# A first stage that sums the modulation as rows from split weights, and output stages with four half buffers

## The chip, the cores and the metric

One kernel on one core of one Trainium2 chip. The metric is the device time of one execution in microseconds (us), and lower is better. Of several runs the median is given. The engines are TensorE (PE, with its weight loads as PEld), VectorE (DVE), ScalarE (ACT), GpSimd (POOL) and SyncE (SP, which here only issues transfers).

## The reference, cut to what matters

Two layers over 1024 latent tokens (x) and 256 context tokens (ctx), all of width 1024 and in fp32. Each layer modulates its input, mixes the tokens, projects back with an output matrix and normalises.

```
silu_c, silu_cc = silu(c), silu(c_ctx)
sh, sc, g = split(silu_c @ mod_w[layer] + mod_b[layer], 3)      # the same for ctx with silu_cc
u = h * (1 + sc) + sh
y = mixer(u)            # layer 0: convolution and mLSTM; layer 1: latent attention
                        # both end in  (...) @ w_out, with w_out (2048, 1024)
h = layer_norm(ALPHA * h + g * y)
```

Layer 0's gates are columns 9216 to 9231 of u @ ev_w_in, plus ev_gate_b.

## The kernel before, in words

Every fp32 product is made of three matmuls on operands split in a high part (the value rounded to F32R) and a low part (value minus high part): high by high, high by low, low by high (mm3, L36 to L42). ACT writes the high part by a copy or an activation that rounds. DVE subtracts and writes the low part over the raw value.

The program is a row of stages: `stage_modulate` (L73), `stage_even` (layer 0's mixer), `stage_out` for layer 0, `stage_latent` and `stage_attend` (layer 1's mixer), `stage_out` for layer 1. A stage ends with a barrier of all engines, so the next begins when the slowest is through. Inside a stage each engine runs its own list of instructions in the order written, and semaphores tie the lists together.

**The first stage** makes u, transposed (1024 features in eight groups k of 128, on the partitions; 1280 tokens along the row), and the gate rows. The tokens lie in three chunks j: 0 holds the 256 context tokens, 1 and 2 hold 512 each. Per k, in the order of PE:
- `columns(k)` (L249): 32 plain fp32 matmuls, with a 128x128 block of mod_w as the stationary operand and two columns of silu as the moving one, give shift and scale of the 128 features. It waits for the slab of mod_w. DVE adds the bias (L201, whose end is the release of all that follows).
- `turn(k)` (L266): ten transposes of the tokens' 128x128 blocks in rotating banks.
- `gates(k-1)` for chunks 1 and 2; those of chunk 0 all come at the end.

ACT applies scale and shift to each transposed chunk and writes u_hi (L166), for chunk 2 also the unrounded u (L168). DVE writes the unrounded u of chunks 0 and 1 (L208), and subtracts to u_lo for all three (L216). After the last gate matmul ACT moves the gate rows out of their banks (`gate_rows`, L174, L175). SP loads mod_w in slabs of 128 columns, two transfers each, into six buffers (L133); ACT issues the ten token tiles of 4 KB rows (L179) ahead of all its own work. `stage_even` then starts with PE projecting tile (0, 0), while ACT waits for the next weights (L540).

**An output stage** computes y = m @ w_out for `count` blocks of 128 tokens (ten in layer 0, eight in layer 1), with 16 blocks of 128 along the sum, so 16 x 2 x 3 = 96 matmuls of 512 columns for each block. The transposed input m is loaded in two halves of eight (L1094), split by ACT (L1166) and DVE (L1214). It has two buffers of 16. The first two blocks go together while w_out arrives in 16 parts (`first_pair`, L1097, L1170, L1218), and every later block n is `project(n)`. A block's load waits until block n-2 is projected (`load_m`). DVE's order is norm(n), then the split of n+2; ACT's is the split of n+2, then `modulate(n)` (L1181; layer 0 only), which empties the banks of PE's `transposes(n)` (L1311). Those come after project(n+1), and after project(2) both 0 and 1. In layer 0 POOL applies gain and bias to the normalised block (L1152, L1154) and stores it.

Of the kernel before, what the change touches and what calls it, by code (L numbers as in the profile page):

```python
# [9 lines left out]
P = 128  # L10
# [62 lines left out]
def stage_modulate(nc, a, keep):  # L73

    SLOTS, TP, R36 = 6, 4, 36
    u_hi, u_lo, mod_col, ident = keep["u_hi"], keep["u_lo"], keep["mod_col"], keep["ident"]
    gate_i, gate_f = keep["gate_i"], keep["gate_f"]
# [4 lines left out]
    PIECES = [(k, j) for k in range(KD) for j in range(3)]  # L82
    piece_at = numbered(PIECES)
    by_dve = numbered(x for x in PIECES if x[1] < 2)
    GATES = (1, 2, 0)
    with ExitStack() as ctx:
        s = Space(nc, ctx, "m")
        u_raw = over(nc, "m_u_raw", [P, KD, T], F32, keep["u_lo_at"])
        x_tok = [s.sb(f"x_tok{n}", [P, D]) for n in range(NT)]
        w = [s.sb(f"w{b}", [P, KD, 2, P]) for b in range(SLOTS)]  # L90
        c_row, c_tanh = s.sb("c_row", [2 * KD, P]), s.sb("c_tanh", [2 * KD, P])
        gw_raw = s.sb("gw_raw", [P, KD, 16])
        gw_hi, gw_lo = s.pair("gw", [P, KD, P])
        g_pre = s.sb("g_pre", [P, 1])
        tp_bank = [s.bank(f"tp{i}") for i in range(TP)]
        col_bank = [s.bank(f"col{i}") for i in range(2)]
        gate_late = [s.bank(f"gate{i}") for i in range(2)]
        gate_bank = [col_bank[0], *gate_late]
        x_in = [s.sem(f"x_in{j}") for j in range(3)]
        w_in = [s.sem(f"w_in{b}") for b in range(SLOTS)]  # L100
        c_in, ident_in, b_in, gw_in, pre_in, first_in = (s.sem(n) for n in ("c_in", "ident_in", "b_in", "gw_in", "pre_in", "first_in"))
        c_t, c_s, c_tp, c_ok, b_ok, ones_ok = (s.sem(n) for n in ("c_t", "c_s", "c_tp", "c_ok", "b_ok", "ones_ok"))
        cols_done, col_ok, tp = (s.sem(n) for n in ("cols_done", "col_ok", "tp"))
        u_hi_ok, u_raw_a, u_raw_d, u_ok = (s.sem(n) for n in ("u_hi_ok", "u_raw_a", "u_raw_d", "u_ok"))
        gw_zero, gw_hi_ok, gw_ok, gate_done, first_hi = (s.sem(n) for n in ("gw_zero", "gw_hi_ok", "gw_ok", "gate_done", "first_hi"))
        w_src = a["mod_w"][0].rearrange("(k p) n -> p k n", p=P)
        h0_src = a["h0"].rearrange("(n p) d -> n p d", p=P)
# [16 lines left out]
        tp_of = lambda k, j: tp_bank[(piece_at[(k, j)] - 1) % TP]  # L124

        @block.sync
        def _(sp):
            def load_slab(k):
                if k >= SLOTS:
                    sp.wait_ge(cols_done, k - SLOTS + 1)  # L130
                for half in range(2):
                    c = D * half + P * k
                    sp.dma_start(w[k % SLOTS][:, :, half, :], w_src[:, :, c:c + P]).then_inc(w_in[k % SLOTS], 16)  # L133
# [4 lines left out]
            load_slab(0)  # L138
            sp.dma_start(b_col[:, :, :], a["mod_b_col"]).then_inc(b_in, 16)
            load_slab(1)  # L140
            sp.dma_start(gw_raw[:, :, :], a["ev_w_in"].rearrange("a (k p) n -> p (a k) n", p=P)[:, :, G0:G0 + 16]).then_inc(gw_in, 16)
            sp.wait_ge(gw_zero, 1)
# [5 lines left out]
            for k in range(2, KD):  # L148
                load_slab(k)
            sp.dma_start(w_first[:, :, :], a["ev_w_in"].rearrange("a (k p) n -> p (a k) n", p=P)[:, :, 4 * D:4 * D + P]).then_inc(first_in, 16)  # L150

        @block.gpsimd
        def _(pool):
            pool.memset(g_pre[:, :], 0.0).then_inc(gw_zero, 1)
            pool.memset(f(gw_hi[:, :, :]), 0.0).then_inc(gw_zero, 1)
            pool.memset(f(gw_lo[:, :, :]), 0.0).then_inc(gw_zero, 1)

        @block.scalar
        def _(act):
# [1997 lines left out]
```

## Time and profile before

| | |
|---|---|
| median of 3 runs | 3075.17 us (3072.52 to 3076.87) |
| the profiled execution | 3071.61 us |
| its span, first to last instruction | 3069.8 us |
| mean granted TensorE clock | 0.972 |
| PE busy | 2917.5 us (95%) |
| DVE, ACT, POOL busy | 1531.2, 1178.5, 234.9 us |
| moved by DMA | 200.79 MB, mean 65 GB/s |

The first stage ends at about 100 us of the span. Layer 0's output stage runs from 1319 to about 1610 us, layer 1's from 2861 us to the end. Overlapping matmuls are shown with their latency, so the cost of one in a stream is the distance from start to start. A granted clock of 1.00 is 2.4 GHz and 0.50 is 1.2 GHz.

### The profile page before, as it was taken

What the parts mean: (1) busy time and instruction counts of PE and PEld (TensorE: products, weight loads), DVE (VectorE), ACT (ScalarE), POOL (GpSimd) and SP (SyncE); (2) the same over time, 40 slices, a digit from 0 to 9 for tenths busy, and PEclk for the clock granted to TensorE, in tenths of its full rate; (3) what the DMA queues carried; (4) which work ended last, traced back from release to release, by engine and by line L of the source; (5) the groups of instructions that cost most, each with busy time, mean ns of one, the idle gap of its engine ahead of it and who ended that gap; (6) DMA issues with size and microseconds to landing.
All of it is one profiled execution on the core that took longest, in us unless ns stands there. A gap on an engine that the chain in (4) does not pass through costs nothing. (4 is left out here: it accounts for less than half of the span.)

```text
span 3069.8 us, 38485 instructions
## 1 busy us (share of the span) xinstructions
PE 2917.5 (95%) x15623; PEld 2505.9 (82%) x15623; DVE 1531.2 (50%) x2791; ACT 1178.5 (38%) x1971; POOL 234.9 (8%) x275
## 2 busy tenths in 40 slices
PE   7999999999999999979979997999999999999798
PEld 7788888888888788857867886888888888887577
DVE  2625652654365535544432323666666656665353
ACT  2423322331233123322234222666666666665310
POOL 0100000000000000002320000202102012020000
PEclk8899999999999999989989998999999999999799
DMA  6311131113111311153341221000100101100432
GB/s 187 93 33 44 45 114 30 44 52 107 30 46 50 107 30 52 33 204 108 121 146 39 90 96 46 26 28 26 32 25 26 36 18 32 31 19 18 175 110 69
DMA packets 223866, 200.79 MB, mean 65 GB/s; under 512 B 12141, under 2 KB 194301, under 8 KB 223690
## 3 DMA queue, kind: packets, MB, share of 16 engines
q1 hardware_dynamic: 207194, 171.28, 18.5%
q0 software_dynamic: 4656, 16.56, 1.4%
q10 hardware_dynamic: 11840, 10.49, 1.0%
q8 instruction: 125, 2.05, 0.3%
q14 instruction: 51, 0.42, 0.1%
HBM read 157.34 MB, written 40.95 MB: 65 GB/s over the span
## 5 line engine op out<-in xcount | busy, mean ns | idle before, releaser
L40 PE MATMUL v_pj<-e_u_hi,e_w_hi 128*128 128x512 f32 (+1 forms) x864 | 308.7, 357 | 1.9 <-PEq L57 1.9
L40 PE MATMUL v_pj<-e_u_hi,v_w_hi 128*128 128x512 f32 (+1 forms) x864 | 308.6, 357 | 0.0
L41 PE MATMUL v_pj<-e_u_lo,v_w_hi 128*128 128x512 f32 (+1 forms) x864 | 306.7, 355 | 0.0
L41 PE MATMUL v_pj<-e_u_lo,e_w_hi 128*128 128x512 f32 (+1 forms) x864 | 306.7, 355 | 0.0
L42 PE MATMUL v_pj<-e_u_hi,v_w_lo 128*128 128x512 f32 (+1 forms) x864 | 306.5, 355 | 0.0
L42 PE MATMUL v_pj<-e_u_hi,e_w_lo 128*128 128x512 f32 (+1 forms) x864 | 306.5, 355 | 0.0
L40 PE MATMUL o_y_bank<-o_w_hi,o_m_hi 128*128 128x512 f32 x576 | 230.9, 401 | 48.8 <-DVE o_w_lo L1218 31.2
L1840 ACT CAST t_pt_hi<-t_ring 128x512 fp32r<-128x512 f32 (+1 forms) x384 | 181.6, 519 | 237.3 <-PE t_ring L2024 237.3
L1925 DVE TENSOR_TENSOR t_pt_lo<-t_ring,t_pt_hi 128x512 fp32r<-128x512 f32 (+1 forms) x384 | 216.2, 598 | 52.8 <-ACT t_pt_hi L1840 51.4
L41 PE MATMUL o_y_bank<-o_w_lo,o_m_hi 128*128 128x512 f32 x576 | 229.0, 398 | 0.0
L42 PE MATMUL o_y_bank<-o_w_hi,o_m_lo 128*128 128x512 f32 x576 | 228.6, 397 | 0.0
L1851 ACT ACTIVATE t_prob<-t_scores,t_bias 128x1280 f32<-128x1280 f32 x128 | 170.6, 1333 | 104.7 <-DVE t_bias L1941 103.9
L40 PEld LDWEIGHTS v_pj<-e_u_hi,v_w_hi 128*128 128x128 f32 x864 | 163.9, 190 | 23.6 <-issue 2.4
L42 PEld LDWEIGHTS v_pj<-e_u_hi,e_w_lo 128*128 128x128 f32 x864 | 163.8, 190 | 23.1
L40 PEld LDWEIGHTS v_pj<-e_u_hi,e_w_hi 128*128 128x128 f32 x864 | 163.9, 190 | 23.0 <-issue 2.1
L42 PEld LDWEIGHTS v_pj<-e_u_hi,v_w_lo 128*128 128x128 f32 x864 | 163.6, 189 | 23.3
L41 PEld LDWEIGHTS v_pj<-e_u_lo,v_w_hi 128*128 128x128 f32 x864 | 164.0, 190 | 21.0
L41 PEld LDWEIGHTS v_pj<-e_u_lo,e_w_hi 128*128 128x128 f32 x864 | 164.0, 190 | 20.6
L1856 ACT ACTIVATE t_prob<-t_prob,t_rec 128x1280 f32<-128x1280 f32 x128 | 177.1, 1384 | 7.4 <-DVE t_rec L1945 7.4
L40 PEld LDWEIGHTS o_y_bank<-o_w_hi,o_m_hi 128*128 128x128 f32 x576 | 111.2, 193 | 75.2 <-DVE o_w_lo L1218 31.9
L40 PE MATMUL l_pj<-l_u_hi,l_w_hi 128*128 128x512 f32 (+3 forms) x376 | 149.8, 399 | 17.2 <-DVE l_u_lo L1530 17.2
L2024 PE MATMUL t_ring<-k_ident,t_prob 128*128 128x128 f32 x1280 | 161.5, 273 | 3.4 <-ACT t_prob L1856 3.4
(380 smaller groups left out, 6446.5 us busy)
## 6 DMA issues: line engine op xcount, KB each, us to landing
e_w_raw<-in_ev_w_in SPq DMA_DIRECT2D x72, 512.0 KB, 4.7
v_mw<-in_mod_w SPq DMA_DIRECT2D x32, 512.0 KB, 4.3
l_w_raw<-in_od_w_in SPq DMA_DIRECT2D x21, 512.0 KB, 4.0
o_m_raw<-mixT SPq DMA_DIRECT2D x20, 512.0 KB, 5.3
m_w<-in_mod_w SPq DMA_DIRECT2D x16, 512.0 KB, 7.7
o_w_raw<-in_ev_w_out SPq DMA_DIRECT2D x16, 512.0 KB, 10.3
zgT<-l_lat_q POOLq DMA_DIRECT2D x16, 512.0 KB, 3.6
t_zg<-zgT SPq DMA_DIRECT2D x32, 256.0 KB, 2.7
```

The source lines that it names most:

```text
L40: nc.tensor.matmul(out, whi, xhi, start=first, stop=False)
L41: nc.tensor.matmul(out, whi, xlo, start=False, stop=False)
L42: return nc.tensor.matmul(out, wlo, xhi, start=False, stop=last)
L1840: nc.scalar.copy(dst, src).then_inc(ring_hi, 1)
L1851: nc.scalar.activation(prob[x][:, :], S[:, 0:T], ACT.Exp, bias=bias[x][:, :], accum_out=total[x][:, :]).then_inc(exp_ok, 1)
L1856: nc.scalar.mul(prob[x][:, :], prob[x][:, :], rec[x][:, :]).then_inc(prob_ok, 1)
L1925: nc.vector.tensor_tensor(dst, src, hi, ALU.subtract).then_inc(ring_free, frees(op))
L2024: last = nc.tensor.transpose(ps[:, c * P:(c + 1) * P], prob[t % 2][:, (c0 + c) * P:(c0 + c + 1) * P], ident[:, :])
```

## The change

First stage. The modulation is now computed as rows. silu is split in high and low (cs, 4 columns: two variants high, two low) and is the stationary operand; the split weights of the slab are the moving one. 16 F32R matmuls of 256 columns give a [4, 256] sum; DVE copies it out, and two small matmuls with a 4x2 selection matrix turn it to columns and add high and low. For that each slab of mod_w (128 x 2048 elements) is split by ACT (`w_high`) and DVE (`w_low`). Slabs come singly at first, then in pairs, over two buffers of a pair. The tokens are loaded by column spans (features 0 to 255, 256 to 511, 512 to 1023), all by SP. u_lo of chunks 0 and 1 is subtracted by POOL. Each chunk has one transpose bank; the gates of chunk 0 run inside the loop. The gate banks stay alive, and `stage_even`'s ACT empties them as its first work.

Output stages. m has four buffers of half a block. Block 2 is loaded when the first half of the first pair is through, block n > 2 when block n-2 is; each split comes one iteration earlier.

```diff
 def stage_modulate(nc, a, keep):
-            for n in range(NT):
-                act.dma_start(x_tok[n][:, :], h0_src[n]).then_inc(x_in[j], 16)
+            def load_slab(k, count):
+                if k >= 4:
+                    sp.wait_ge(r_done, k - 2)
+                for half in range(2):
+                    c = D * half + P * k
+                    sp.dma_start(w_raw[(k // 2) % 2][:, :, half, P * (k % 2):P * (k % 2) + P * count], w_src[:, :, c:c + P * count]).then_inc(w_in[arrival(k)], 16)
...
+            load_slab(0, 1)
+            sp.dma_start(sel[:, :], a["c_sel"]).then_inc(sel_in, 16)
+            sp.dma_start(b_col[:, :, :], a["mod_b_col"]).then_inc(b_in, 16)
+            load_x(0)
+            load_slab(1, 1)
...
+            load_slab(2, 2)
+            load_x(1)
+            load_slab(4, 2)
+            load_x(2)
+            load_slab(6, 2)
...
         @block.gpsimd
+            for k in range(KD):
+                for j in (1, 0):
+                    pool.wait_ge(u_raw_d, by_dve[(k, j)])
+                    pool.wait_ge(u_hi_ok, piece_at[(k, j)])
+                    pool.tensor_tensor(u_lo[:, k, span(j)], u_raw[:, k, span(j)], f(u_hi[:, k, span(j)]), ALU.subtract).then_inc(u_lo_p, 1)
...
         @block.scalar
+            def u(k):
+                act.wait_ge(col_ok, k + 1)
+                high(k, 1)
+                high(k, 2)
+                whole(k, 2)
+                high(k, 0)
+            def w_high(k):
+                act.wait_ge(w_in[arrival(k)], 32)
+                if k >= 2:
+                    act.wait_ge(r_done, k - 1)
+                nc.scalar.copy(high_of(k), slab(w_raw, k)).then_inc(w_hi_ok, 1)
...
+            w_high(0)
+            u(0)
+            w_high(1)
...
+            w_high(2)
+            for k in range(1, KD):
+                u(k)
+                if k + 2 < KD:
+                    w_high(k + 2)
...
         @block.vector
+            row_sums(0)
             for k in range(KD):
                 columns(k)
                 whole(k, 0)
                 whole(k, 1)
...
+                else:
+                    if k + 1 < KD:
+                        row_sums(k + 1)
+                    low(k, 2)
+                    if k + 2 < KD:
+                        w_low(k + 2)
...
         @block.tensor
+            def row_sums(k):
+                pe.wait_ge(w_lo_ok, k + 1)
...
+                for kk in range(KD):
+                    nc.tensor.matmul(sums, cs[:, kk, :], high_of(k)[:, kk, :, :], start=kk == 0, stop=False)
+                    last = nc.tensor.matmul(sums, cs[:, kk, :], slab(w_lo, k)[:, kk, :, :], start=False, stop=kk == KD - 1)
+                last.then_inc(r_done, 1)
...
+            def turn(k, j):
...
+                if k:
+                    if j == 2:
+                        pe.wait_ge(u_raw_a, k)
+                    elif j == 1:
+                        pe.wait_ge(u_raw_d, by_dve[(k - 1, 1)])
+                    else:
+                        pe.wait_ge(u_hi_ok, piece_at[(k - 1, 0)])
...
+            for k in range(KD):
+                row_sums(k)
+                for j in ORDER:
+                    turn(k, j)
+                if k:
+                    for j in ORDER:
+                        gates(k - 1, j)
+                columns(k)
+            for j in ORDER:
+                gates(KD - 1, j)
 def stage_even(nc, a, keep):
+            for j, bank in enumerate((x_bank, y_bank, z_bank)):
+                gate_rows(j, bank)
             act.wait_ge(const_in, 16)
 def stage_out(nc, a, keep, layer):
-    YB = 3
+    YB, SLOTS = 3, 4
+    HALVES = [(0, 0), (1, 0), (0, 1), (1, 1)] + [(n, h) for n in range(2, count) for h in range(2)]
+    order_of = numbered(HALVES)
+    slot = lambda n, h: (order_of[(n, h)] - 1) % SLOTS
...
             def load_m(n, h):
-                b = n % 2
-                if n >= 2:
-                    sp.wait_ge(y_half, half_at[(n - 2, 1)])
+                b = slot(n, h)
+                if n == 2:
+                    sp.wait_ge(first_half, 1)
+                if n > 2:
+                    sp.wait_ge(y_half, half_at[(max(n - 2, 1), 1)])
...
             for n in range(count):
+                if n + 3 < count:
+                    load_m(n + 3, 0)
+                    load_m(n + 3, 1)
                 if n + 2 < count:
-                    load_m(n + 2, 0)
-                    load_m(n + 2, 1)
                     load_res(n + 2)
...
             for n in range(count):
                 norm(n)
-                if n + 2 < count:
-                    split(n + 2, 0)
-                    split(n + 2, 1)
+                if n + 3 < count:
+                    split(n + 3, 0)
+                    split(n + 3, 1)
...
+                    if k == H - 1:
+                        last.then_inc(first_half, 1)
```

## Rows read from the trace of the kernel before

**Rows 1.** The page's busy time, share and instructions of each engine.
```profile
PE 2917.5 (95%) x15623; PEld 2505.9 (82%) x15623; DVE 1531.2 (50%) x2791; ACT 1178.5 (38%) x1971; POOL 234.9 (8%) x275
```
**Rows 2.** Stretches: length, busy and count per engine, granted clock, DMA share, GB/s.
```profile
30.00:40.00 10.00, 10.00 (x44) 9.61 (x45) 4.20 (x10) 3.74 (x6) 0.00 (x0) 1.00 1.20 291
...
50.00:60.00 10.00, 10.00 (x44) 9.52 (x44) 2.66 (x6) 2.79 (x4) 0.00 (x0) 0.50 0.00 0
```
**Rows 3.** First stage in order of time: start, length, instruction [idle before, releaser].
```profile
20.27 6.96 PE L249 MATMUL m_col<-k_c_silu,m_w 128*128 128x2 f32 x32 [11.86 <-DMA m_w<-in_mod_w]
...
36.11 0.16 DVE L201 TENSOR_TENSOR k_mod_col<-m_col,k_b_col 128x4 f32<-128x4 f32 x1 [4.31 <-PE m_col L249]
...
89.04 2.37 PE L266 MATMUL m_tp<-k_ident,m_x_tok 128*128 128x128 f32 x10
89.21 0.16 DVE L201 TENSOR_TENSOR k_mod_col<-m_col,k_b_col 128x4 f32<-128x4 f32 x1 [3.83 <-PE m_col L249]
```
**Rows 4.** First stage by line and form: count, busy us, mean ns, idle before.
```profile
L249 PE MATMUL m_col<-k_c_silu,m_w 128*128 128x2 f32 x256 | 40.9, 295 | 11.9 <-DMA m_w<-in_mod_w 11.9
...
L166 ACT ACTIVATE e_u_hi<-m_tp,k_mod_col 128x512 fp32r<-128x512 f32 x16 | 12.5, 778 | 2.9 <-PE m_tp L266 2.3
...
L168 ACT ACTIVATE m_u_raw<-m_tp,k_mod_col 128x512 f32<-128x512 f32 x8 | 6.2, 770 | 0.0
...
L166 ACT ACTIVATE e_u_hi<-m_tp,k_mod_col 128x256 fp32r<-128x256 f32 x8 | 4.5, 565 | 42.9 <-PE m_tp L266 42.9
```
**Rows 5.** Order of time, matmuls of 256 columns, last two gates, then stage_even.
```profile
98.29 0.28 PE L41 MATMUL m_col<-e_u_lo,m_gw_hi 128*128 128x256 f32 x1
...
98.41 0.28 PE L42 MATMUL m_col<-e_u_hi,m_gw_lo 128*128 128x256 f32 x1
...
100.60 0.36 PE L40 MATMUL v_pj<-e_u_hi,e_w_hi 128*128 128x256 f32 x1 [1.91 <-PEq L57]
...
102.00 0.41 PE L40 MATMUL v_pj<-e_u_hi,e_w_hi 128*128 128x256 f32 x1
...
102.21 0.41 PE L41 MATMUL v_pj<-e_u_lo,e_w_hi 128*128 128x256 f32 x1
```
**Rows 6.** Input tile of the output stages: count, min/median/max ns, first and last start.
```profile
L1166 ACT CAST o_m_hi<-o_m_raw x36: 1040/1053/1060, 1323.6 to 3022.8; 128x1024 fp32r<-128x1024 f32 x36
L1214 DVE TENSOR_TENSOR o_m_lo<-o_m_raw,o_m_hi x36: 1216/1226/3423, 1324.7 to 3023.9; 128x1024 fp32r<-128x1024 f32 x36
```
**Rows 7.** POOL by line and form: count, busy us, mean ns, idle before.
```profile
L1803 POOL TENSOR_TENSOR t_turn<-t_turn,t_part 128x512 f32<-128x512 f32 x16 | 20.5, 1281 | 24.8 <-DVE t_part L1911 23.7
```
**Rows 8.** ACT in order of time, its first work on weights in stage_even.
```profile
105.85 1.05 ACT L540 CAST v_w_hi<-e_w_raw 128x1024 fp32r<-128x1024 f32 x1 [2.81 <-DMA e_w_raw<-in_ev_w_in]
```
**Rows 9.** Layer 0's output stage, PE in order of time, two starts and their streams.
```profile
1383.04 0.79 PE L40 MATMUL o_y_bank<-o_w_hi,o_m_hi 128*128 128x512 f32 x1 [5.59 <-DVE o_m_lo L1214]
...
1388.30 0.40 PE L40 MATMUL o_y_bank<-o_w_hi,o_m_hi 128*128 128x512 f32 x1
...
1407.13 0.40 PE L42 MATMUL o_y_bank<-o_w_hi,o_m_lo 128*128 128x512 f32 x1
...
1414.20 0.76 PE L40 MATMUL o_y_bank<-o_w_hi,o_m_hi 128*128 128x512 f32 x1 [2.51 <-DVE o_m_lo L1214]
...
1419.01 0.39 PE L42 MATMUL o_y_bank<-o_w_hi,o_m_lo 128*128 128x512 f32 x1
```
**Rows 10.** Layer 1's output stage, PE in order of time, start of project(2).
```profile
2927.56 0.79 PE L40 MATMUL o_y_bank<-o_w_hi,o_m_hi 128*128 128x512 f32 x1 [7.38 <-DVE o_m_lo L1214]
...
2931.35 0.40 PE L40 MATMUL o_y_bank<-o_w_hi,o_m_hi 128*128 128x512 f32 x1
```
**Rows 11.** Layer 0's output stage, DVE: norm(1), first and last instruction.
```profile
1384.13 0.69 DVE L1233 TENSOR_TENSOR o_y<-o_y_bank,o_g_bc 128x512 f32<-128x512 f32 x1
...
1389.50 0.81 DVE L1243 TENSOR_SCALAR o_y<-o_y,o_mean_var,o_rstd 128x1024 f32<-128x1024 f32 x1 [0.94 <-POOL o_rstd L1143]
```
**Rows 12.** Input of both output stages: issue to landing.
```profile
DMA to landing us min/median/max: 3.9/5.3/13.3
```

More of the change, by code:

```diff
@@ L88, in stage_modulate @@
         u_raw = over(nc, "m_u_raw", [P, KD, T], F32, keep["u_lo_at"])
-        x_tok = [s.sb(f"x_tok{n}", [P, D]) for n in range(NT)]
-        w = [s.sb(f"w{b}", [P, KD, 2, P]) for b in range(SLOTS)]
+        x_tok = s.sb("x_tok", [P, NT, D])
+        w_hi = [s.sb(f"w_hi{b}", [P, KD, 2 * P], F32R) for b in range(2)]
+        w_lo, w_raw = [], []
+        for b in range(2):
+            at = next_offset(nc)
+            w_lo.append(s.sb(f"w_lo{b}", [P, KD, 2, 2 * P], F32R))
+            w_raw.append(over(nc, f"m_w_raw{b}", [P, KD, 2, 2 * P], F32, at))
@@ L91, in stage_modulate @@
         c_row, c_tanh = s.sb("c_row", [2 * KD, P]), s.sb("c_tanh", [2 * KD, P])
+        cs = s.sb("cs", [P, KD, 4], F32R)
+        sel = s.sb("sel", [4, 2])
+        rows = s.sb("rows", [4, 2 * P])
         gw_raw = s.sb("gw_raw", [P, KD, 16])
         gw_hi, gw_lo = s.pair("gw", [P, KD, P])
[L94 to L102, printed above, removed]
+        tp_bank = keep["pj"]
+        x_bank, y_bank, z_bank, col_bank = keep["banks"]
@@ L242, in columns @@
             def columns(k):
-                b = k % SLOTS
-                pe.wait_ge(w_in[b], 32 * (k // SLOTS + 1))
-                if k >= 2:
-                    pe.wait_ge(col_ok, k - 1)
+                pe.wait_ge(rows_ok, k + 1)
+                if k:
+                    pe.wait_ge(col_ok, k)
                 for half in range(2):
-                    for kk in range(KD):
-                        last = nc.tensor.matmul(col_bank[k % 2][:, 2 * half:2 * half + 2], w[b][:, kk, half, :], c_silu[:, kk, :],
-                                                start=kk == 0, stop=kk == KD - 1)
+                    last = nc.tensor.matmul(col_bank[:, 2 * half:2 * half + 2], rows[0:4, P * half:P * half + P], sel[0:4, :], start=True, stop=True)
@@ L1057, in stage_out @@
         m_hi, m_lo, m_raw = [], [], []
-        for b in range(2):
-            m_hi.append(s.sb(f"m_hi{b}", [P, KM, P], F32R))
+        for b in range(SLOTS):
+            m_hi.append(s.sb(f"m_hi{b}", [P, H, P], F32R))
             m_at = next_offset(nc)
-            m_lo.append(s.sb(f"m_lo{b}", [P, KM, P], F32R))
-            m_raw.append(over(nc, f"o{layer}_m_raw{b}", [P, KM, P], F32, m_at))
+            m_lo.append(s.sb(f"m_lo{b}", [P, H, P], F32R))
+            m_raw.append(over(nc, f"o{layer}_m_raw{b}", [P, H, P], F32, m_at))
         res = [s.sb(f"res{b}", [P, D]) for b in range(2)]
@@ L1208, in _ @@
         def _(dve):
[L1209 removed]
             def split(n, h):
[L1212 to L1214 removed]
+                b = slot(n, h)
+                dve.wait_ge(m_hi_ok, order_of[(n, h)])
+                nc.vector.tensor_tensor(m_lo[b][:, :, :], m_raw[b][:, :, :], f(m_hi[b][:, :, :]), ALU.subtract).then_inc(m_ok, 1)
             def split_w(k):
@@ L1257, in _ @@
                 split_w(k)
+            split(2, 0)
+            split(2, 1)
             if layer == 0:
@@ L1269, in _ @@
                 norm(n)
-                if n + 2 < count:
-                    split(n + 2, 0)
-                    split(n + 2, 1)
+                if n + 3 < count:
+                    split(n + 3, 0)
+                    split(n + 3, 1)
         @block.tensor
```

225 lines of the change are left out of this document (120 added, 105 removed).

## The prediction

> **What bounds the kernel now.** I read the page's engine line first: PE is busy for 95% of the span [rows 1], so only stretches in which PE stands still, runs slowly, or does work that could be shorter are worth anything. The diff touches the first stage and the two output stages, and I read those in windows, in order of time and by line.
>
> In the first stage PE looks full: 10.00 of 10.00 us in both windows [rows 2]. It isn't at its peak there. The clock is 0.50 from 50 to 60 us, and 256 matmuls of two columns take 40.9 us [rows 4], for a result of four numbers per feature. The stage has a beginning, a period and a tail. The first matmul on mod_w starts at 20.27 us, after waiting 11.86 us for its slab, because ten token tiles share the DMA engines with it [rows 3]. DVE's modulation column is ready at 36.27 us for group 1 and at 89.37 us for group 7 [rows 3], six periods of 8.85 us. The last gate matmul starts at 98.41 us and the next stage's first at 100.60 us [rows 5].
>
> In an output stage the matmuls follow each other closely but for a few places, which the order of time shows. Project(2) starts 5.59 us late in layer 0 and 7.38 us late in layer 1, each time released by the split of its input [rows 9, 10]: the load of block 2 may only start when the first pair is through. Project(3) in layer 0 waits another 2.51 us [rows 9]. After each gap PE runs at half clock for a while.
>
> **The step lengths of PE.** Between 1388.30 and 1407.13 us project(2) issues 83 of its 96 matmuls of 512 columns, 0.227 us each at 2.4 GHz. Its first 12 take 5.26 us from 1383.04, 0.438 each at 1.2 GHz [rows 9]. With 256 columns the distance is 0.12 us at the fast level and 0.21 at the slow one [rows 5].
>
> **First stage, the new period.** Count from the moment when the column of group k is ready. Two chains run to the same moment of group k+1.
>
> The chain of ACT and DVE: u(k) on ACT is two of 0.778, one of 0.770 and one of 0.565, 2.89 us [rows 4]. Then w_high(k+2): the trace has no copy of 2048 elements, so I take two of 1024, 2 x 1.053 = 2.11 [rows 6] (below: one fixed cost less, perhaps 0.2 less; above: a strided write could cost more, bounded at twice). Then w_low(k+2) on DVE, 2 x 1.226 = 2.45 [rows 6], and DVE's column, 0.16 [rows 3]. w_low stands ahead of columns(k+1) in DVE's list, so the column waits for it even though nothing needs that slab yet. Sum 7.6, with hand-overs 7.7 us.
>
> The chain of PE: 16 row sums of 256 columns, 1.9 us fast or 3.4 slow; ten transposes, 2.37 [rows 3]; gates of all three chunks, 6 x 0.227 + 3 x 0.12 = 1.7 fast, 6 x 0.438 + 3 x 0.21 = 3.3 slow; two small matmuls and their hand-overs, for which I take 0.6 (nearest rows: 0.295 each for L249 [rows 4]; none below zero, at most 1). Sum 6.6 us fast, 9.7 slow.
>
> Which clock? In the old loop PE fell to 0.50 although it was never idle [rows 2], in a loop of two-column matmuls and transposes. The new one keeps the transposes but has 25 wide matmuls per period in place of six. I expect it to change level inside each period, row sums and columns fast, gates slow: 1.9 + 2.4 + 3.3 + 0.6 = 8.2 us. That is above the 7.7 of the other chain, so the period is 8.2 us, and its bounds are 7.7 and 9.7.
>
> POOL's subtractions take 1.28 us for 512 elements [rows 7], and about 0.65 for 256. They start when DVE and ACT have written their inputs, some 2 us into the period, and end by about 4, ahead of w_low at 5. I cost them at nothing; their cover is that gap. If they fell beside w_low it would cost: the same kind of DVE subtraction has a median of 1.226 us and a maximum of 3.423 [rows 6]. The Trainium skill ("SBUF — State Buffer", "Who interferes with whom") says that a VectorE instruction with two inputs in SBUF and a GpSimd one that reads SBUF exclude each other, the later one waiting for the whole of the earlier. By that rule all of POOL's 1.9 us could join DVE's chain; this is a rival below, priced from the rows.
>
> **Start.** Slab 0 now comes first, 1 MB. Mod_w moves at 291 GB/s in the 30 to 40 us window [rows 2], 3.6 us of transfer, so it is there at about 7.5 to 8 instead of 20.27. Then in series: w_high 2.1, w_low 2.45, row sums slow 3.4, copy 0.4, transposes, the two small matmuls and DVE's column 3.2. The column of group 0 is ready near 19.3. From there u(0) 2.9, w_high(1) 2.1, w_low(1) 2.45, row sums 3.4, transposes 2.4, gates 3.3, small ones 0.6 give 36.5. So the early start is spent by group 1, which stood at 36.27 before: splitting a slab is on the path until slabs are split ahead. If PE were fast in these steps it would be 33.
>
> Column 7: 36.5 + 6 x 8.2 = 85.7 us, against 89.37. The loads don't hold it: 13.6 MB at 291 GB/s take 47 us, and the last pair of slabs, let go by row sums 3 at about 47, is needed at 62.
>
> **Tail.** ACT's and DVE's writes of group 7 end 1.8 us after the column for chunk 1, POOL needs 1.3 more, then the gates 1.7 to 3.3: 5.6 us on average, and 0.9 for the barrier. Before, 24 gate matmuls of chunk 0 and the evacuations by ACT stood here. These six evacuations move to stage_even. There ACT waited 2.81 us for a load before its first weights at 105.85, 5.3 us after the stage began [rows 8, 5], and their 3.7 us fit in. New start of stage_even: 85.7 + 5.6 + 0.9 = 92.2, against 100.6. **8.4 us saved** (0 at a period of 9.7; 16 at 7.7 with the fast start).
>
> **Output stages.** Block 2 is loaded from the middle of the first pair, some 22 us ahead of its use; the transfer takes 5.3 us [rows 12], and ACT and DVE split it behind the last weights. Gaps gone: 5.6 and 7.4 us. With them goes the slow restart: 5.26 - 12 x 0.227 = 2.5 us in layer 0; 9 matmuls in 3.79 us, 3.79 - 2.04 = 1.8 us in layer 1 [rows 9, 10]. Project(3) in layer 0: its split no longer stands behind modulate(0), 2.5 us gone; its slow restart cost 4.81 - 11 x 0.227 = 2.3 us, but the transposes ahead of it stay, and I count half, 1.2. Layer 0 gives 11.8 us, layer 1 9.2. **21.0 us saved.**
>
> What is queued anew: DVE now does norm(n+1) behind the split of block n+3, which waits for a load let go at the end of project(n+1). 5.3 for the load, 2.1 and 2.5 for the splits, 5.4 + 0.8 for the norm [rows 11, 12] are 16 us after project(n+1), and PE's transposes of it come 21.8 us after. SP's order puts the store of layer 1 behind the load as well, with blocks to spare. Both cost nothing as long as the load is not late.
>
> **Sum.** 8.4 + 21.0 = 29.4 us. Against the profiled execution's own time, 3071.6 - 29.4 = 3042.2. The median of the runs is 3.6 above it, so I give 3045.6 us.
>
> **Rivals.**
> - PE at 1.2 GHz through the whole first stage: the period is 9.7 and the stage gains nothing. For it: 0.50 in a window of the old loop [rows 2]. Against: there are four times as many wide matmuls. 3054 us, chance 0.18.
> - PE at 2.4 GHz throughout: period 7.7, start at 33. 16 us there, 37 in all, 3038 us, chance 0.14.
> - POOL beside w_low, by the page's rule: 7.7 + 1.9 = 9.6 instead of 8.2, 6 x 1.4 = 8 us lost. For it: the maximum of 3.423 [rows 6]. Against: the order inside the period. 3054 us, chance 0.08.
> - The change in the output stages gives less than it says: block 2 is early, but a clock drop or a late split replaces the gap, and only about 10 of 21 us come. 3057 us, chance 0.06.
> - Slower: the load of m lands late in layer 0's output stage. At the longest landing of 13.3 us [rows 12] norm ends at 24, 2.3 us after PE wants it, and PE waits and restarts slowly (2.5) at seven blocks: 34 us, more than the 29.4 gained, 3079 us. It decides once a load takes over 11 us in the steady part. Against: that figure falls while the weights stream in; the median is 5.3. Chance 0.03.
>
> My forecast keeps 0.51. The range takes in the first four and the spread of the runs: 3036 to 3057. What a measurement can tell from no change is about 0.2%, 6 us: faster 0.94, same 0.03, slower 0.03.
>
> **What would show it.** In order of time: the first row sums near 12 us, columns of groups 1 and 7 near 36 and 86, stage_even's first matmul near 92. A period of 9.7 with spacing 0.21 in the row sums means the slow clock; a w_low over 3 us means POOL. In the output stages no idle time on DVE's split at project(2), DVE's norm ahead of PE's transposes. I am wrong if w_high takes much over 2.1 us, if slab 0 lands after 10, or if PE waits for norm.

## The result, and the profile after

The changed kernel takes **3029.87 us** (median of 4 runs, 3028.97 to 3032.92), the kernel before 3074.06 us on the same chip (4 runs). The ratio is 0.9857, 95% interval 0.984 to 0.9874. The profiled execution took 3030.1 us, its span is 3028.3 us, 41.5 less than before. The forecast was 3045.6 us with a range of 3036 to 3057: the direction was right, and the gain was half as large again as I had worked out.

To see where it came from, I cut both spans at the first matmul of each stage:

| stage (us) | before | after | gained | forecast |
|---|---|---|---|---|
| first stage, to stage_even's first matmul | 100.6 | 79.5 | 21.1 | 8.4 |
| stage_even | 1228.5 | 1232.0 | -3.5 | 0 |
| output stage, layer 0 | 267.0 | 254.4 | 12.6 | 11.8 |
| latent and attention stages | 1275.8 | 1271.7 | 4.1 | 0 |
| output stage, layer 1 | 197.9 | 190.7 | 7.2 | 9.2 |

Stage_even measured 1227.9 to 1233.8 us and the latent and attention stages 1271.7 to 1277.8 in the twelve traces of this case, whichever of the two versions they ran, so the two entries of 3.5 and 4.1 us say nothing about the change. (The end of layer 0's output stage, given ahead of the prediction as about 1610 us, is earlier: the next stage's first matmul starts at 1596.1.) The output stages came as forecast within 1.2 us together. The first stage gave 12.7 us more than I said. All that follows is about that.

The page's engine line answers to [rows 1]. PE is 33 us less busy, and the work on DVE stays the same in sum:

```profile
PE 2884.8 (95%) x15527; PEld 2468.4 (82%) x15527; DVE 1531.3 (51%) x2792; ACT 1190.3 (39%) x1980; POOL 249.6 (8%) x291
```

The windows of the changed kernel answer to [rows 2]. After the length stand the busy time and count of PE, PEld, DVE, ACT and POOL, then the granted clock, the DMA share and GB/s:

```profile
20.00:30.00 10.00, 5.86 (x30) 4.40 (x31) 5.94 (x8) 4.03 (x6) 1.58 (x2) 0.66 0.64 195
30.00:40.00 10.00, 8.79 (x62) 6.66 (x61) 7.01 (x10) 5.63 (x7) 2.43 (x2) 1.00 1.08 373
...
50.00:60.00 10.00, 7.80 (x57) 6.02 (x56) 7.98 (x9) 5.23 (x7) 2.43 (x2) 1.00 0.03 7
60.00:70.00 10.00, 8.89 (x63) 6.89 (x61) 8.30 (x11) 7.02 (x9) 4.71 (x4) 1.00 0.01 2
```

PE is *less* busy than before (7.80 of 10 us against 10.00) and yet stands at a clock of 1.00 from 30 to 70 us, where it had fallen to 0.50. Around that stretch the clock was low twice, each time after PE had stood idle: from 22 us on, in a wait of 6.97 us for w_low(1), and for the gates of the tail below, after one of 3.33 us. DVE's column of groups 0 to 7 starts at 17.20, 31.74, 38.55, 45.34, 52.15, 58.94, 65.75 and 71.64 us: a start, five equal periods of 6.80 and one of 5.89.

One period in order of time, from column 1 to column 2 (the columns of the view are those of [rows 3]):

```profile
31.74 0.16 DVE L250 TENSOR_TENSOR k_mod_col<-e_e,k_b_col 128x4 f32<-128x4 f32 x1 [1.38 <-PE e_e L320]
...
31.94 1.45 ACT L196 ACTIVATE e_u_hi<-e_pj,k_mod_col 128x512 fp32r<-128x512 f32 x2 [7.91 <-DVE k_mod_col L250]
...
33.71 2.43 POOL L187 TENSOR_TENSOR e_u_lo<-m_u_raw,e_u_hi 128x512 fp32r<-128x512 f32 x2 [12.13 <-DVE m_u_raw L259]
...
33.78 1.29 PE L336 MATMUL e_pj<-k_ident,m_x_tok 128*128 128x128 f32 x10
...
34.09 1.45 DVE L264 TENSOR_TENSOR e_u_lo<-m_u_raw,e_u_hi 128x512 fp32r<-128x512 f32 x1
34.39 1.92 ACT L213 CAST m_w_hi<-m_w_raw 128x2048 fp32r<-128x2048 f32 x1
...
36.34 2.29 DVE L240 TENSOR_TENSOR m_w_lo<-m_w_raw,m_w_hi 128x2048 fp32r<-128x2048 f32 x1 [0.80 <-ACT m_w_hi L213]
...
38.55 0.15 DVE L250 TENSOR_TENSOR k_mod_col<-e_e,k_b_col 128x4 f32<-128x4 f32 x1
...
38.74 0.78 ACT L196 ACTIVATE e_u_hi<-e_pj,k_mod_col 128x512 fp32r<-128x512 f32 x1 [2.43 <-DVE k_mod_col L250]
```

Read the starts, and the chain of ACT and DVE closes without a gap: u(k) from 31.94 to 34.39, w_high to 36.34, w_low to 38.55, column and hand-over to 38.74. That is 2.45 + 1.95 + 2.21 + 0.19 = 6.80 us. The column has no idle time before it: PE's small matmuls had been done since 37.6, and DVE reached it only after w_low. PE is not on this chain.

The tail, in order of time, answers to [rows 5]:

```profile
71.64 0.16 DVE L250 TENSOR_TENSOR k_mod_col<-e_e,k_b_col 128x4 f32<-128x4 f32 x1 [0.42 <-PE e_e L320]
...
74.93 0.79 PE L40 MATMUL e_y<-e_u_hi,m_gw_hi 128*128 128x512 f32 x1 [3.33 <-POOL e_u_lo L187]
75.52 0.63 PE L41 MATMUL e_y<-e_u_lo,m_gw_hi 128*128 128x512 f32 x1
...
78.08 0.41 PE L42 MATMUL e_x<-e_u_hi,m_gw_lo 128*128 128x256 f32 x1
...
79.50 0.55 PE L40 MATMUL e_pj<-e_u_hi,e_w_hi 128*128 128x256 f32 x1 [1.01 <-PEq L57]
```

In the output stages the view of PE's waits shows what is left. Layer 0 (engine, who waits for whom: us in total, times, longest):

```profile
PE o_y_bank L40 <- DVE o_w_lo L1313: 16.4, 1, 16.4
...
PE o_t_bank L1410 <- DVE o_y L1338: 3.4, 1, 3.4
PE o_t_bank L1410 <- ACT o_u_out L1276: 2.0, 2, 1.3
PE o_y_bank L40 <- DVE o_m_lo L1309: 1.3, 1, 1.3
```

and layer 1:

```profile
PE o_y_bank L40 <- DVE o_w_lo L1313: 12.7, 1, 12.7
PE o_y_bank L40 <- DVE o_m_lo L1309: 2.5, 1, 2.5
```

The waits for o_m_lo at project(2), 5.59 and 7.38 us in [rows 9, 10], are gone. What is left on it (1.3 and 2.5) belongs to the stage's second matmul, while w_out arrives. Project(3) in layer 0 follows its transposes directly and at the fast clock, where [rows 9] had 2.51 us of idle time and a slow restart:

```profile
1384.99 0.66 PE L1410 MATMUL o_t_bank<-k_ident,o_y 128*128 128x128 f32 x4 [0.68 <-ACT o_u_out L1276]
1385.40 0.47 PE L40 MATMUL o_y_bank<-o_w_hi,o_m_hi 128*128 128x512 f32 x1
1385.71 0.39 PE L41 MATMUL o_y_bank<-o_w_lo,o_m_hi 128*128 128x512 f32 x1
1385.94 0.40 PE L42 MATMUL o_y_bank<-o_w_hi,o_m_lo 128*128 128x512 f32 x1
```

### The profile page after: what moved, and what is told of

Read it like the earlier page. It is cut to its first block and busy times, and to the rows that moved or that the text cites. A ratio compares the mean times of both kernels' runs of the same rounds, so it can differ in the third digit from the quotient of the medians.

```text
span 3028.3 us, 38367 instructions
## 1 busy us (share of the span) xinstructions
PE 2884.8 (95%) x15527; PEld 2468.4 (82%) x15527; DVE 1531.3 (51%) x2792; ACT 1190.3 (39%) x1980; POOL 249.6 (8%) x291
## 5 line engine op out<-in xcount | busy, mean ns | idle before, releaser
L40 PE MATMUL e_pj<-e_u_hi,e_w_hi 128*128 128x512 f32 (+1 forms) x864 | 309.5, 358 | 1.0 <-PEq L57 1.0
L40 PE MATMUL e_pj<-e_u_hi,v_w_hi 128*128 128x512 f32 (+1 forms) x864 | 309.1, 358 | 0.0
L41 PE MATMUL e_pj<-e_u_lo,e_w_hi 128*128 128x512 f32 (+1 forms) x864 | 307.5, 356 | 0.0
L42 PE MATMUL e_pj<-e_u_hi,e_w_lo 128*128 128x512 f32 (+1 forms) x864 | 307.3, 356 | 0.0
L41 PE MATMUL e_pj<-e_u_lo,v_w_hi 128*128 128x512 f32 (+1 forms) x864 | 307.0, 355 | 0.0
L42 PE MATMUL e_pj<-e_u_hi,v_w_lo 128*128 128x512 f32 (+1 forms) x864 | 306.8, 355 | 0.0
L42 PEld LDWEIGHTS e_pj<-e_u_hi,e_w_lo 128*128 128x128 f32 x864 | 164.6, 191 | 23.1
L40 PEld LDWEIGHTS e_pj<-e_u_hi,e_w_hi 128*128 128x128 f32 x864 | 164.9, 191 | 22.2 <-issue 1.3
L41 PEld LDWEIGHTS e_pj<-e_u_lo,e_w_hi 128*128 128x128 f32 x864 | 164.8, 191 | 20.6
L41 PEld LDWEIGHTS e_pj<-e_u_lo,v_w_hi 128*128 128x128 f32 x864 | 164.3, 190 | 21.0
```

Of the source, the lines that this page charges most:

```text
L40: nc.tensor.matmul(out, whi, xhi, start=first, stop=False)
L41: nc.tensor.matmul(out, whi, xlo, start=False, stop=False)
L42: return nc.tensor.matmul(out, wlo, xhi, start=False, stop=last)
```

## The experiments

The ratios are to the kernel before, run on the same chip. "first" is the start of stage_even's first matmul. e4 and e7 ran once each, so their times have no interval, and they are read from their traces. Beside the changed kernel ten others ran:

| run | us, median | ratio, 95% | first | output 0 / 1 |
|---|---|---|---|---|
| after | 3029.87 | 0.9857 (0.984 to 0.9874) | 79.5 | 254.4 / 190.7 |
| e1, first stage alone | 3053.23 | 0.9925 (0.991 to 0.9941) | 81.1 | 266.9 / 199.3 |
| e2, output stages alone | 3051.97 | 0.9929 (0.9916 to 0.9943) | 97.5 | 256.6 / 190.0 |
| e3, w_low after the column | 3059.31 | 0.9954 (0.9941 to 0.9966) | 108.6 | 252.4 / 191.1 |
| e4, 32 two-column matmuls more | 3118.0 (one run) | | 164.5 | 252.2 / 190.0 |
| e5, DVE subtracts for POOL | 3032.59 | 0.9864 (0.9849 to 0.9879) | 79.2 | 252.6 / 189.5 |
| e6, w_high a slab further ahead | 3029.54 | 0.9861 (0.9844 to 0.9877) | 79.5 | 254.3 / 190.6 |
| e7, 16 two-column matmuls more | 3058.05 (one run) | | 110.3 | 254.1 / 189.9 |
| e8, tokens loaded first | 3046.66 | 0.9914 (0.99 to 0.9929) | 95.8 | 254.4 / 190.7 |
| e9, block 2 loaded late | 3048.58 | 0.992 (0.9905 to 0.9935) | 79.3 | 264.3 / 199.4 |
| e10, e5 and e6 together | 3027.95 | 0.9855 (0.9839 to 0.9872) | 77.4 | 254.0 / 189.3 |

### The halves: e1 and e2

e1 is the changed kernel with the old `stage_out`, e2 the old kernel with the new one.

```diff
 e1
-def stage_out(...):   # the changed one, whole
+def stage_out(...):   # the one of before, whole
 e2
-def stage_out(...):   # the one of before, whole
+def stage_out(...):   # the changed one, whole
```

> The new first stage with the old output stages. Theory (the two parts don't touch each other, and the first stage was the mis-sized term): stage_even's first matmul at 79.5 us of the span as in the changed kernel, the gaps of 5.6 and 7.4 us at project(2) are back, and the time is 21 us below the kernel before, less some 3 us for slow clock in stage_even: 3053 to 3056 us. Rival (my forecast's size of the first stage was right and the rest came from elsewhere): about 3066 us.

> The old first stage with the new output stages. Theory: the output stages give what the prediction summed for them, 21 us, give or take 3: 3050 to 3056 us, stage_even starting at 100.6. Rival (the output stages gave the surplus): 3040 us or less, since then 35 us would be theirs.

Both times came as expected, though stage_even began at 81.1 us in e1 (expected 79.5) and at 97.5 in e2 (expected 100.6). e1 gains 20.8 us over the 3074.01 of before and e2 gains 22.0. Together 42.8, beside the 44.2 of both: the parts add up, and neither needs the other. e2 also shows how far the old first stage moves by itself, 97.5 against 100.6: in its trace the periods are 8.25 to 8.4 throughout, while the trace of before has one of 11.4, in which the granted clock stayed at 0.50 (the window from 50 to 60 us in [rows 2]). So some 3 of the 21.1 us are an episode of the old trace, and the first stage is worth about 18 to 21.

### Is w_low in front of the column a loss? e3

In the changed kernel the column waits for w_low of a slab that is needed later. e3 puts it behind.

```diff
                 columns(k)
                 whole(k, 0)
                 whole(k, 1)
...
                 else:
                     if k + 1 < KD:
+                        w_low(k + 1)
                         row_sums(k + 1)
                     low(k, 2)
-                    if k + 2 < KD:
-                        w_low(k + 2)
```

> The changed kernel, with w_low(k+1) placed behind the modulation column and the unrounded u of group k in DVE's list, where it stood ahead of that column one group earlier. Theory (the chain through ACT's u, w_high and DVE's w_low sets the period of 6.80 us): the column no longer waits for w_low, and the period falls to what DVE's or PE's own work needs, 5.8 to 6.2 us, so stage_even starts 4 to 6 us earlier and the time falls by as much, to about 3025. Rival (PE's chain sets it): the period stays 6.8 and the time the same.

It missed: 3059.31 us, 29 slower than the changed kernel, with periods of 10.9 to 12.3. In order of time, the third group:

```profile
44.96 2.28 DVE L240 TENSOR_TENSOR m_w_lo<-m_w_raw,m_w_hi 128x2048 fp32r<-128x2048 f32 x1
45.13 3.94 POOL L187 TENSOR_TENSOR e_u_lo<-m_u_raw,e_u_hi 128x512 fp32r<-128x512 f32 x2 [7.13 <-DVE m_u_raw L259]
...
47.30 0.38 PE L309 MATMUL e_z<-m_w_hi,m_cs 128*4 128x256 f32 x1 [4.18 <-DVE m_w_lo L240]
...
51.26 0.67 DVE L264 TENSOR_TENSOR e_u_lo<-m_u_raw,e_u_hi 128x512 fp32r<-128x512 f32 x1
```

Nothing is ahead any more. PE stands idle for 4.18 us until w_low is there and then runs its row sums 0.21 us apart. The whole loop is a circle: column, w_low, row sums, copy, small matmuls, column. In the changed kernel w_low(k+2) costs the column 2.2 us and buys PE the whole period. I had called it a wait that "nothing needs"; it is the look-ahead that keeps PE out of the chain. The POOL row shows the contention that I had as a rival, the other way round: w_low came first and took its 2.28 us, and POOL's two subtractions, begun behind it, took 3.94 instead of 2.43: some 2.1 us until w_low's end, and then their own time.

### What took the clock down in the old loop? e4 and e7

Both add fp32 matmuls of two columns, the kind that the change removed, to each group, and write to columns of the bank that nothing reads.

```diff
             def columns(k):
...
+                for m in range(32):     # e7: range(16)
+                    nc.tensor.matmul(col_bank[:, 64:66], ident[:, :], c_silu[:, m % KD, :], start=m == 0, stop=m == 31)
```

> The changed kernel with 32 plain fp32 matmuls of two columns (identity by silu, into a spare part of the column bank) ahead of each group's two small matmuls, as many as the old loop had. They add PE work and keep PE busier. Theory (that work is what took the clock down in the old loop): the matmuls of 512 columns in the loop go back to 0.43 us apart, ten transposes to 2.4 us, and the period to 11 us or more. Rival (PE being busy is enough for the fast clock): 0.227 us apart, transposes 1.3 us, and a period of 5.5 + 32 x 0.125 = 9.5 us.

> The changed kernel with 16 plain fp32 matmuls of two columns ahead of each group's small ones: the old loop's true number, which the trace shows as 32 instructions (the run with 32 showed 64). Theory (a row of such matmuls takes the clock down although PE is busy): row sums and transposes of the next group at the slow clock, period 11 to 12 us, stage_even at about 115. Rival (fast clock, the matmuls only add their time): 5.5 + 4.0 = 9.5 us a period, stage_even at about 100.

First a correction that these runs brought. The text ahead of the prediction calls `columns(k)` 32 matmuls. The code issues 16 (two halves by eight); the trace lists each fp32 matmul of this kind as two instructions, so x32 there. e7 is the old number, e4 twice that. Their rows, e4 first:

```profile
43.77 8.89 PE L320 MATMUL e_e<-k_c_silu,k_ident 128*128 128x2 f32 x64
...
56.90 2.33 PE L338 MATMUL e_pj<-k_ident,m_x_tok 128*128 128x128 f32 x10
```

and e7:

```profile
50.34 0.38 PE L311 MATMUL e_z<-m_w_hi,m_cs 128*4 128x256 f32 x1
50.51 0.41 PE L312 MATMUL e_z<-m_w_lo,m_cs 128*4 128x256 f32 x1
50.73 0.41 PE L311 MATMUL e_z<-m_w_hi,m_cs 128*4 128x256 f32 x1
...
53.71 1.29 PE L338 MATMUL e_pj<-k_ident,m_x_tok 128*128 128x128 f32 x10
...
56.60 3.63 PE L320 MATMUL e_e<-k_c_silu,k_ident 128*128 128x2 f32 x32
```

with one of its windows of 10 us (those from 30 to 100 us have the same clock):

```profile
50.00:60.00 10.00, 10.00 (x71) 8.39 (x70) 4.82 (x6) 4.36 (x5) 1.96 (x2) 0.83 0.52 161
```

In e7 PE is never idle in these windows, and the granted clock is 0.83 in every one where the changed kernel has 1.00. The two-column matmuls take 3.63 us, and *behind* them the row sums stand 0.21 us apart (1.2 GHz) until the transposes, which with the gates run fast again: 3.37 + 2.89 + 3.63 and hand-overs are the period of 10.4. The theory had 11 to 12 because it expected slow transposes too; its rival's 9.5 had a fast clock throughout, which is refuted. In e4 the period is 17.16, of which the 64 instructions take 8.89, and even the transposes are slow (2.33 for 1.29); the gates, expected slow, were fast again (0.23 us apart). Here the two-column matmuls are the only thing added, so they are what lowers the clock. It was not how busy PE is: 10.00 busy goes with 0.83 in e7, 7.80 with 1.00 in the changed kernel, and 10.00 with 1.00 in the changed kernel from 90 to 120 us, in stage_even.

The old loop's own trace shows the same. One of its groups, and the stretches on both sides of the fall (the view of the windows as above):

```profile
60.41 3.72 PE L249 MATMUL m_col<-k_c_silu,m_w 128*128 128x2 f32 x32
63.99 2.38 PE L266 MATMUL m_tp<-k_ident,m_x_tok 128*128 128x128 f32 x10
```

```profile
60.45:63.85 3.40, 3.40 (x33) 3.40 (x32) 0.00 (x0) 0.00 (x0) 0.00 (x0) 1.00 0.02 5
63.90:67.25 3.35, 3.35 (x15) 3.16 (x15) 1.60 (x4) 2.19 (x4) 0.00 (x0) 0.50 0.00 0
```

From 43 to 90 us its clock falls from 1.00 to 0.50 five times, each time in the second half of such a row of two-column matmuls or as it ends, with PE never idle. That is the 0.50 of [rows 2]. The row itself takes 3.72 us at 1.00 (60.41) and 6.82 at 0.50 (49.00). So removing them paid twice, by their own length and by the speed of what stands behind them.

A warning on the clock column: it reads 1.00 in 30:40 of [rows 2], but two gate matmuls of 512 columns in that window start at 38.54 and 38.96 us, 0.42 apart, which is the slow distance. The same holds for the changed kernel's row sums from 12.3 to 14.9 us, 0.21 apart under a figure of 1.00. In both traces the column becomes believable only later, from about 40 and 15 us. The distance of the matmuls decides.

### Does POOL's help pay, and what bounds a group? e5, e6, e10

e5 gives POOL's two subtractions per group to DVE. e6 runs ACT's w_high one slab further ahead, so that w_low no longer waits for it. e10 does both.

```diff
 e5, e10
-            for k in range(KD):   # @block.gpsimd, subtractions of chunks 1 and 0
+            def low_own(k):       # @block.vector, the same two, called first in low(k, 2)
 e6, e10
             w_high(2)
+            w_high(3)
             for k in range(1, KD):
                 u(k)
-                if k + 2 < KD:
-                    w_high(k + 2)
+                if k + 3 < KD:
+                    w_high(k + 3)
```

> The changed kernel with the subtractions of u_lo for chunks 0 and 1 given back from POOL to DVE, ahead of that of chunk 2. Theory (DVE has room before ACT's w_high ends, and while POOL subtracts, DVE's own subtraction of chunk 2 takes 1.23 to 1.45 us where it takes 0.67 with POOL quiet): the period stays 6.8 us within 0.1, and the time the same within 1 us. Rival (POOL's help is part of the gain): the period grows by DVE's added 1.1 us, to 7.9, and the time by 6 to 8 us.

> The changed kernel with ACT's w_high one slab further ahead: w_high(3) in the idle time before group 1, then w_high(k+3) behind u(k) in place of w_high(k+2). DVE's list stays. Theory (the period of 6.80 is u on ACT 2.45, w_high 1.92, w_low 2.2 and the column in series): w_low(k+2) finds its high part ready and starts right behind the subtraction of chunk 2, the chain is cut by ACT's 1.9 us, and DVE's own work of some 5.9 us sets the period: stage_even starts 5 us earlier, at 74 to 75, and the time is 3025. Rival (a wait of DVE for PE or for the loads takes its place): the period stays above 6.5 and the time within 1.5 us of the changed kernel's.

> The changed kernel with two earlier edits joined: POOL does no subtraction (VectorE takes the 128x512 and the 128x256 of each group) and ScalarE's copy of the weights to their high part runs one slab further ahead. Theory (VectorE's own list is now the bound of a group): the sum of its list is 0.27 column, 0.55 + 0.27 + 0.81 + 0.30 whole parts, 0.30 row sums, 1.0 + 0.65 low parts, 2.29 w_low = 6.4 us, so the period of a group is 6.4 to 6.5 us, the same as with POOL beside it (6.46), and the kernel is within 2 us of the changed kernel (0.4 us x 5 groups at most gained). Rival (in the run one slab ahead it was POOL's contention that took the gain away: low part 1.23 for 0.67 and w_low 2.83 for 2.29, 1.1 us a group): with POOL quiet the period falls to 5.9 or below and stage_even starts 3 to 4 us earlier, 3026 us.

In e5 the period is 6.80 as before, and the median of 3032.59 us (3028.02 to 3034.68) can't be told from the changed kernel's: POOL's subtractions sat beside DVE's own wait for ACT, and moving them changes nothing. With POOL quiet DVE's subtraction of 512 elements is faster:

```profile
48.95 0.67 DVE L266 TENSOR_TENSOR e_u_lo<-m_u_raw,e_u_hi 128x512 fp32r<-128x512 f32 x1
```

against 1.45 in the row at 34.09 of the changed kernel. And where DVE is busy elsewhere, as in e7, POOL's pair is shorter than the 2.43 us of the row at 33.71:

```profile
52.42 1.96 POOL L187 TENSOR_TENSOR e_u_lo<-m_u_raw,e_u_hi 128x512 fp32r<-128x512 f32 x2 [8.40 <-DVE m_u_raw L259]
```

Of these 1.96 us the 128x512 takes 1.27 (its mean in e7 and in the changed kernel alike) and the 128x256 the other 0.69. With that the changed kernel's group can be followed: POOL's first one runs from 33.71 to 34.98, DVE's (begun at 34.09) would need 0.67 more and ends at 35.54, POOL's second begins behind that and ends at 36.14, 0.60 later. By these ends the three run one after the other, though two engines do them, and whichever comes later waits for the other. This agrees with the Trainium skill ("SBUF — State Buffer", "Who interferes with whom"), by whose rule the two exclude each other.

e6 shows it on the path. Its theory failed: stage_even began at 79.5 us, not at 74 to 75, and the median did not move. The first column came 1.5 us and the second 2.1 us later than in the changed kernel (the edit touches neither; column 0 starts between 17.2 and 18.7 us in the runs that leave the start alone), and the periods won back only 1.7: they fell to 6.46 and no further, because w_low now started while POOL was at work:

```profile
48.74 2.42 POOL L187 TENSOR_TENSOR e_u_lo<-m_u_raw,e_u_hi 128x512 fp32r<-128x512 f32 x2 [4.03 <-DVE m_u_raw L260]
...
49.28 1.28 DVE L265 TENSOR_TENSOR e_u_lo<-m_u_raw,e_u_hi 128x512 fp32r<-128x512 f32 x1
50.49 2.82 DVE L241 TENSOR_TENSOR m_w_lo<-m_w_raw,m_w_hi 128x2048 fp32r<-128x2048 f32 x1
```

w_low takes 2.82 us, ending 0.53 later than its 2.29 would, and POOL's row ends at 51.16. In e10 POOL is quiet. Its periods are 6.06 to 6.26 with one of 7.41, in which ACT waited 3.28 us for a slab to land. The others lie between the theory (6.4 to 6.5, DVE's own list) and the rival (5.9 or below), and DVE's list has no idle time on ACT's w_high any more:

```profile
46.64 1.00 DVE L261 TENSOR_TENSOR e_u_lo<-m_u_raw,e_u_hi 128x512 fp32r<-128x512 f32 x2
47.57 0.67 DVE L267 TENSOR_TENSOR e_u_lo<-m_u_raw,e_u_hi 128x512 fp32r<-128x512 f32 x1
48.17 2.27 DVE L236 TENSOR_TENSOR m_w_lo<-m_w_raw,m_w_hi 128x2048 fp32r<-128x2048 f32 x1
50.38 0.14 DVE L246 TENSOR_TENSOR k_mod_col<-e_e,k_b_col 128x4 f32<-128x4 f32 x1
```

Stage_even begins at 77.4 us, 2.1 earlier, and the median is 3027.95, which with these intervals can't be told from the changed kernel. Once ACT's wait is removed, DVE's list bounds these groups, and no such move of work between the three gained more here.

### The early slab: e8

```diff
+            for q in range(3):
+                load_x(q)
             load_slab(0, 1)
...
-            load_x(0)
...
-            load_x(1)
...
-            load_x(2)
```

> The changed kernel with all nine token transfers issued ahead of slab 0 of mod_w, about the order of bytes that the kernel before had. Theory (everything up to the first column is in series behind slab 0): slab 0 lands some 13 us later, at about 21, the first column comes at 30, and stage_even starts 11 to 13 us later; 3042 us. Rival (my prediction: the early start is spent by group 1 anyway): 0 to 3 us later, 3031 us.

All tokens are loaded ahead of mod_w, as before the change. The first rows that matter:

```profile
22.81 1.90 ACT L212 CAST m_w_hi<-m_w_raw 128x2048 fp32r<-128x2048 f32 x1 [18.66 <-DMA m_w_raw<-in_mod_w]
...
33.05 0.16 DVE L249 TENSOR_TENSOR k_mod_col<-e_e,k_b_col 128x4 f32<-128x4 f32 x1 [1.78 <-PE e_e L319]
```

w_high(0) starts at 22.81 instead of 7.79, and every column and stage_even itself come 16 us later, with the same periods of 6.80. The median is 3046.66 us, 16.8 more: the theory's 3042 was too low, and its rival of 0 to 3 us is refuted. In the kernel before the slab was used at 20.27 us, 2.5 earlier than in e8. So the early slab is worth 12 to 16 of the 21 us, and everything else that changed in the stage together 5 to 9, of which 3 are the episode of the old trace. What each of those other changes is worth alone was not tested.

### The output stages: e9

```diff
-                if n == 2:
-                    sp.wait_ge(first_half, 1)
-                if n > 2:
+                if n >= 2:
                     sp.wait_ge(y_half, half_at[(max(n - 2, 1), 1)])
```

> The changed kernel, with one wait moved: in the output stages the load of token block 2 waits, as block 3's does, until the y halves of block 1 are stored away (the end of the first pair), instead of until the first half of the first projection. Buffers, the order of TensorE, the norms and the joined buffers stay new. Theory (the gaps at project(2) were nothing but block 2 landing late, and the rest of the gain stands by itself): a gap of 5 to 8 us before project(2)'s first matmul comes back in both layers with its slow restart of 2 to 2.5 us, the output stages measure about 262 and 198 us in place of 254 and 191, and the kernel takes about 3045 us (3041 to 3049). Rival 1 (project(3)'s slow transposes and restart hang on the same late load, by a shift of the whole schedule): the output stages are back at 267 and 198 and the kernel takes about 3053. Rival 2 (the new order covers the late load): no gap over 2 us and a time within 4 us of the changed kernel.

3048.58 us, 18.7 more than the changed kernel, with the output stages at 264.3 and 199.4. PE's waits in layer 0 and the restart of project(2):

```profile
PE o_y_bank L40 <- DVE o_m_lo L1307: 7.7, 2, 6.4
```

```profile
1361.96 0.79 PE L40 MATMUL o_y_bank<-o_w_hi,o_m_hi 128*128 128x512 f32 x1 [6.44 <-DVE o_m_lo L1307]
...
1366.25 0.39 PE L41 MATMUL o_y_bank<-o_w_lo,o_m_hi 128*128 128x512 f32 x1
...
1390.30 0.63 PE L41 MATMUL o_y_bank<-o_w_lo,o_m_hi 128*128 128x512 f32 x1
```

One line moved brings back 9.9 of layer 0's 12.6 us, and 8.7 in layer 1, where the whole change had gained 7.2. In layer 0 that is the gap of 6.44 us; the ten matmuls from 1361.96 to 1366.25, 4.29 us for 2.27; and some 1.7 us because project(3)'s first matmuls are slow again (0.63 us long at 1390.30), although it no longer waits for its input. So the early load of block 2 is most of the change in this stage. The other 2.7 us fit the wait of 2.51 us that the split one iteration earlier removes. The theory's 3045 was a little low for the median and right for the parts; the rival that all of it would come back was wrong in layer 0, while its remark that project(3)'s slow restart hangs on the same load was right.

## Why the prediction missed

**What held.** PE's two kinds of gaps in the output stages and their slow restarts were sized at 21.0 us and measured 19.8. Layer 0 gave 12.6 for 11.8: I had counted half of project(3)'s slow restart, and all of it went. Layer 1 gave 7.2 for 9.2: the gap and the restart went, but the stage's second matmul waited 2.5 us for its input where it had waited 0.9. DVE's norm behind the split cost nothing, as I had said: norm(2) ended at 1395.8, some 11 us before PE wanted it. The rival of a late m did not show. The evacuations moved to stage_even cost nothing that a trace shows.

**What failed is the size of the first stage**, 21.1 us for 8.4. By the steps:

- *Column 0*, forecast ready at 19.3, measured 17.36 (its row starts at 17.20). Over half of the difference is the ten transposes: 1.25 us, where I took 2.37. That row [rows 3] ran at the slow clock (0.50 from 89.04 to 91.41 us), and I used it as if it held at either level.
- *Column 1*, forecast 36.5, measured 31.90. From column 0 it is 14.54 us instead of 17.2. The row sums were slow, as I had said (24.14 to 27.51), but the gates behind them were fast, 1.7 us for 3.3, and the transposes took 1.90 for the 2.4 of the sum.
- *The period*, forecast 8.2, measured 6.80 five times and 5.89 once: 39.9 us for 49.2. This is the main failure, and it has two parts. The clock: I let PE drop to 1.2 GHz in the gates of each group, since the old loop had dropped "although it was never idle". I took a busy PE and its clock together and counted on the transposes, which the new loop keeps, to lower it again. e7 shows that it was the two-column matmuls, the very thing the change removes. That is 6 x (8.2 - 7.7) = 3.0 us, and it is the rival of 2.4 GHz throughout, to which I had given 0.14. The chain of ACT and DVE: forecast 7.7, measured 6.80, and 5.4 us over six periods. I had added durations where the trace shows starts. ACT's instructions overlap, so u(k) is 2.45 us from start to start and not 2.89, and w_high and w_low of 2048 elements are 1.95 and 2.21, less than twice those of 1024. The last period has no w_low in front of its column, which I charged all the same: 0.9 us.
- *The tail*, forecast 6.5, measured 7.70 from the end of column 7 at 71.80. POOL's subtraction let the gates start 3.13 us after it (forecast 3.1); they ran at the slow clock all the way, 3.15 us from the first start to the last, after PE had been idle for 3.33 us; I had taken 2.5, the mean of both levels. The barrier took 1.4 for 0.9.

4.6 earlier at column 1, 9.3 earlier over the periods, 1.2 later in the tail are the 12.7 us. With -1.2 for the output stages and 0.6 for the stages in between these are the 12.1 us between my 29.4 and the 41.5 of the two spans. The last 3.6 us of the miss are the step from profile to median: before, the profiled execution lay 3.6 us below the median, and I carried that over (as 3.4: by the sum, 3042.2 + 3.6, the forecast should have read 3045.8), but after the change it lies 0.2 above it (3030.1 and 3029.87).

**The reading of the start** was half right. I compared column 1 after with column 1 before, found them equal, and concluded that the early slab was spent. Measured, the first slab was used 12.5 us earlier (7.79 for 20.27) and column 1 was ready 4.4 us earlier (31.90 for 36.27). So 8.1 us did go into longer first two groups, most of it into splitting their slabs. But spent is not worthless: what the early slab is worth has to be read against the changed kernel without it. That is e8, and it is 16 us.

**POOL** cost nothing, as in my sum, but by a margin of 0.2 us: it ended at 36.14, and w_low began at 36.34. Its own prices were right (1.27 and 0.69 for 1.28 and 0.65). The contention that I had as a rival, with a chance of 0.08, did occur, only against DVE's subtraction of chunk 2 instead of w_low, and there DVE still had 0.80 us to wait for ACT. I had looked for it in one place of DVE's list alone.

## What to carry to other kernels

Cost a chain by starts, not by durations, and take every PE duration together with the granted clock of its own window, checked against the distance from matmul to matmul. When PE runs slowly while it looks full, ask what *kind* of matmul fills it before expecting the same clock of a new loop: in e7 two-column fp32 matmuls took a third of the loop and slowed what followed. The worth of an early load, or of an instruction issued ahead, shows only when it alone is taken away; the early slab and the w_low of a later group both looked idle on paper, and the kernel took 17 and 29 us more without them.

## What the runs showed of the hardware

- A granted clock of 0.83 went with PE 10.00 of 10 us busy in e7, and 1.00 with 7.80 of 10 in the changed kernel. Sixteen fp32 matmuls of two columns per group were the whole difference in PE's work. They take 3.63 us in e7 at a granted clock of 1.00; those of the old loop, with weights that change at each, took 3.72 at 1.00 and 6.82 at 0.50.
- A trace of this case lists one fp32 matmul of two columns as two instructions (16 in the code, x32 in the trace), and one fp32 transpose of 128x128 as one (ten, x10).
- Ten fp32 transposes of 128x128 on PE took 1.25 to 1.29 us at the fast level, 2.33 (e4) to 2.38 (the kernel before, 63.99) at 0.50, and 1.90 where the clock rose in between.
- DVE's and POOL's subtractions of SBUF operands behave as if they excluded each other, and the trace shows the wait inside the duration, not as idle time: DVE's of 128x512 took 0.67 us alone and 1.23 to 1.45 beside POOL's; POOL's pair took 1.96 alone, 2.43 beside DVE's 128x512 and 3.94 beside DVE's 128x2048.
